# A two-layer streaming encoder step in float32: request packs of two pairs instead of one, and layer inputs that arrive already turned

## The reference

```python
for l in range(DEPTH):                         # 2 layers, for prompt and for requests
    P = rmsnorm(x, g_norm[l]) @ w_in[l]        # 1024 channels in
    o_a = sparse attention: an indexer keeps the top 256 (requests: 132) keys
    o_b = forgetting attention: logit[t,s] += F[t]-F[s], causal
    o_c = attention in a band of 8+1 chunks of 64, learned bias
    o_m = cross-attention into 256 memory tokens, kv = rmsnorm(mem, g_mem[l]) @ w_mem_kv[l]
    x = x + concat(o_a, o_b, o_c, o_m, each * silu(its gate)) @ w_out[l]
y = rmsnorm(x, g_final)                        # new keys and values are outputs too
```

## Time and profile before

| | us |
|---|---|
| median of 3 runs | 1713.91 |
| lowest, highest | 1713.59, 1715.81 |
| the profiled execution's own time | 1712.33 |
| its span, first to last instruction | 1710.5 |
| PE busy | 1692.7 |
| DVE busy | 1005.7 |
| ACT busy | 662.3 |
| POOL busy | 239.7 |

### The profile page before, as it was taken

How to read it: one execution, slowest core, us unless ns; L and a number is a source line. 1 busy time by engine, 2 the same in 40 slices (tenths; PEclk the granted TensorE clock), 3 DMA queues, 4 the chain that set the end, 5 groups by cost and what they waited for, 6 DMA issues and landing times.

```text
span 1710.5 us, 30251 instructions
## 1 busy us (share of the span) xinstructions
PE 1692.7 (99%) x10866; PEld 1103.7 (65%) x10866; DVE 1005.7 (59%) x2707; ACT 662.3 (39%) x1599; POOL 239.7 (14%) x452
## 2 busy tenths in 40 slices
PE   9999999999999999999999999999999999999998
PEld 4466677767778755555444677767777886555553
DVE  3645888778878333333235378887888772333321
ACT  4532334333343345454124323343333433445531
POOL 1233321100010010002012433220000001000000
PEclk9999999999999999999999999999999999999999
DMA  8344322223132322114421533231231324221130
GB/s 285 94 143 126 127 94 87 97 78 106 41 134 94 103 79 97 40 47 115 129 94 51 166 104 127 94 137 44 81 109 38 132 97 121 69 90 37 46 108 37
DMA packets 60340, 166.64 MB, mean 97 GB/s; under 512 B 11345, under 2 KB 29745, under 8 KB 57889
## 3 DMA queue, kind: packets, MB, share of 16 engines
q1 hardware_dynamic: 43584, 125.88, 23.0%
q0 software_dynamic: 16608, 38.83, 6.9%
HBM read 137.03 MB, written 30.73 MB: 98 GB/s over the span
## 4 chain that ended last, share of the span: by engine, by line
PE 80%; DVE 14%; DMA 2%; issue 2%; ACT 1%; DVEq 1%; ACTq 0%; SPq 0%
PE psX L876 54%; DVE lower L1268 9%; PE psT L816 7%; PE psX L1052 6%; PE psS L985 6%; DVE work L1490 2%; PE psS L904 2%; DMA wring<-in_w 2%; PE psS L816 1%; PE psX L816 1%; PE psX L1027 1%; DVE gate L1322 0%; PE psS L954 0%; PE psS L924 0%; DVE sc L1434 0%
## 5 line engine op out<-in xcount | busy, mean ns | idle before, releaser
L876 PE MATMUL psX<-wring,hT 128*128 128x512 f32 (+2 forms) x2016 | 834.3, 557 | 6.4 <-ACT kv L1146 3.0
L876 PEld LDWEIGHTS psX<-wring,hT 128*128 128x128 f32 x2016 | 363.9, 190 | 327.5 <-issue 318.6
L1268 DVE TENSOR_SCALAR_CACHE_REDUCE lower<-sc,thr 128x640 uint8<-128x640 f32 (+5 forms) x462 | 407.3, 934 | 17.5 <-issue 9.5
L876 PE MATMUL psX<-hT,wring 128*128 128x128 f32 x2880 | 334.6, 275 | 0.9 <-ACT gate L1166 0.4
L876 PEld LDWEIGHTS psX<-hT,wring 128*128 128x128 f32 x2880 | 327.7, 192 | 3.6 <-issue 3.0
L1208 ACT ACTIVATE work<-work,stat 128x256 f32<-128x256 f32 (+7 forms) x288 | 200.0, 694 | 295.9 <-DVEq L1493 293.3
L1217 ACT COPY work<-psT 128x512 f32<-128x512 f32 (+2 forms) x352 | 156.7, 488 | 321.0 <-PE psT L816 319.7
L816 PEld LDWEIGHTS psT<-con,work 128*128 128x128 f32 x1080 | 121.4, 141 | 73.2 <-issue 66.5
L816 PE MATMUL psT<-con,work 128*128 128x128 f32 x1080 | 158.2, 278 | 0.0
L1490 DVE CUSTOM_DVE_ANT_0 work<-psS,bias 128x640 f32<-128x640 f32 (+7 forms) x120 | 86.2, 718 | 41.9 <-issue 20.5
L1490 DVE CUSTOM_DVE_ANT_0 work<-psS,sc 128x384 f32<-128x384 f32 (+5 forms) x48 | 42.8, 891 | 72.1 <-PE psT L816 70.0
(11 more groups left out here) (203 smaller groups left out, 1537.9 us busy)
## 6 DMA issues: line engine op xcount, KB each, us to landing
wring<-in_w SPq DMA_DIRECT2D x17, 2048.0 KB, 9.4
cache<-in_kB SPq DMA_DIRECT2D x16, 512.0 KB, 7.0
cache<-in_vB SPq DMA_DIRECT2D x16, 512.0 KB, 4.1
cache<-in_kC SPq DMA_DIRECT2D x16, 512.0 KB, 6.8
cache<-in_vC SPq DMA_DIRECT2D x16, 512.0 KB, 4.7
scratch_oscr<-gate POOLq DMA_DIRECT2D x54, 128.0 KB, 2.0
hT<-scratch_oscr SPq DMA_DIRECT2D x18, 384.0 KB, 3.6
kv<-in_x SPq DMA_DIRECT2D x9, 512.0 KB, 5.7
```

The source lines that it names most:

```text
L876: mm = pe.matmul(out, lhs, rhs, start=(kt == 0), stop=(kt == KT - 1))
L1268: v.tensor_scalar(lower[:, at:at + STRIP_L[t]], sc[:, o], thr[:, n:n + 1], 0.0, ALU.is_lt, ALU.add, accum_out=below[:, n:n + 1])
```

## The change

Two things are changed.

First, a request pack now holds two pairs, requests four at a time: pair `j` goes to the first score buffer and pair `j+1` to the second, as even and odd heads do for the prompt. There are two request packs a branch instead of four; scores, values and `om` are written for both in one step, the queries of both pairs are prepared in one step on POOL, and the cache loads carry an index `i` for the pair. `sbias_` stays one buffer, so that between the two `L` of a B or A pack it is loaded anew.

Second, x of layer 0 and the memory tokens of both layers come a second time from the host, transposed (`xT`, `memT`), straight into `hT` and `memT`. There `norm` multiplies the turned tile by the gain per channel (DVE), and `turn` is one PE transpose of the reciprocal roots, spread over 128 columns, by which DVE multiplies the turned tile. The plain tiles are still loaded for the squares. The turned loads are `XT` steps of SP: x tiles 0, 1, 2, then 3 and 4, then 5 to 8, then the memory (6 in layer 0, one in layer 1). The two broadcast gain loads of 512 KB in layer 0, and one in layer 1, go.

```diff
+TURNED_IN = {"x0": range(0, 1), "x1": range(1, 2), "x2": range(2, 3), "x3": range(3, 5), "x5": range(5, 9), "m": range(9, 11)}
+def comes_turned(l, n):
+    return l == 0 or n > ST_
 def heads(pack):
-    return 1 if is_sample(pack) else pack[3]
+    return pack[3]
...
     emit("X", ("x", 0))
     emit("ident")
-    emit("gn")
+    emit("XT", "x0")
     emit("head")
     emit("X", ("x", 1))
+    emit("XT", "x1")
     emit("W", "A1")
+    emit("gm")
     emit("con")
     emit("X", ("x", 2))
+    emit("XT", "x2")
     emit("X", ("x", 3))
-    emit("gm")
+    emit("XT", "x3")
+    emit("XT", "x5")
     emit("W", "mm")
+    emit("XT", "m")
     emit("norm", 0)
...
                 queue += packs_of(c[0], t)
-                j = t
-                if c != "A2" and j < PAIRS:
-                    queue.append((c[0], f"s{j}", j, 1))
-        queue += [("A", f"s{j}", j, 1) for j in range(PAIRS)]
+                if c != "A2" and t in (1, 3):
+                    queue.append((c[0], f"s{t - 1}", t - 1, 2))
+        queue += [("A", f"s{j}", j, 2) for j in range(0, PAIRS, 2)]
...
-        gone = (l, ("turn", t)) if kind != "r" else (l + 1, ("turn" if l + 1 < DEPTH else "y", t))
+        gone = (l, ("norm", t)) if kind != "r" else (l + 1, ("turn" if l + 1 < DEPTH else "y", t))
...
         if l:
             put(at[(l, ("P", "A1", 0))], l, "gm")
+            put(at[(l, ("P", "A1", 0))], l, "XT", "m")
...
+                elif k == "XT":
...
+                        cols = slice(group[0] * P, (group[-1] + 1) * P)
+                        src = d["xT"].rearrange("p (k c) -> p k c", k=KT)
+                        sp.dma_start(hT[:, :, cols], src[:, :, cols]).then_inc(xT_loaded[s[1]].sem, 16)
...
+                    if comes_turned(l, n):
+                        turn(S.ap(s)[:, 0:P], rstd[:, 2, n:n + 1].to_broadcast([P, P])).then_inc(S.fill(s).sem, 1)
+                        continue
...
+                    if comes_turned(l, n):                       # DVE, norm
...
+                        dve.wait_ge(*xT_loaded[x].on(x))
+                        v.tensor_tensor(turned_tile(n), turned_tile(n), con[:, c0:c0 + KT].unsqueeze(2).to_broadcast([P, KT, P]),
+                                        ALU.mult)
+                        dve.wait_ge(*rooted.on(n))
+                        v.reciprocal(rstd[:, 2, n:n + 1], rstd[:, 1, n:n + 1]).then_inc(normed.sem, 1)
...
+                    if comes_turned(l, n):                       # DVE, turn
+                        roots = S.ap(s)[:, 0:P].unsqueeze(1).to_broadcast([P, KT, P])
+                        v.tensor_tensor(turned_tile(n), turned_tile(n), roots, ALU.mult).then_inc(S.empty(s).sem, 1)
...
+                elif k == "L" and is_sample(s[1]):               # POOL
...
+                    if br == "B":
+                        pool.wait_ge(*logits.on((p, i)))
...
+                        sample_bias(*sbias_loads[j + 1])
+                        if i == 0:
+                            close_samples("B", j + 1)
+                    elif br in "CA" and j + 1 < PAIRS:
+                        pool.wait_ge(*logits.on((p, i)))
+                        if br == "C":
+                            close_samples("C", j + 1)
+                        else:
+                            sample_bias("A", j + 1)
```

More of the change, by code:

```diff
@@ L172, in advance @@
             emit("S", pack)
-            if is_sample(pack) and pack[2] + 1 < PAIRS:
-                j = pack[2] + 1
-                emit("Q", (pack[0], f"s{j}", j, 1))
+            if is_sample(pack) and pack[2] + 2 < PAIRS:
+                j = pack[2] + 2
+                emit("Q", (pack[0], f"s{j}", j, 2))
         if prev:
@@ L205, in settle @@
             emit("V", pipe[1])
-        if old and is_sample(old) and old[2] == PAIRS - 1:
+        if old and is_sample(old) and old[2] + old[3] == PAIRS:
             emit("R", old[0])
@@ L411, in cache_uses @@
         elif s[0] in ("S", "V") and is_sample(s[1]):
-            out += [(l, (s, "k" if s[0] == "S" else "v", r)) for r in parts(s[1][0])]
+            out += [(l, (s, "k" if s[0] == "S" else "v", (i, r))) for i in range(s[1][3]) for r in parts(s[1][0])]
     return out
@@ L609, in encoder @@
         half_loaded = Signal(sem("half_of_b1_loaded"), [(l, "B1") for l in range(DEPTH)], lambda e: 16)
-        h_act = Signal(sem("hT_by_act"), events(["turn"], lambda s: s[1]))
+        h_act = Signal(sem("hT_by_act"), [(l, s[1]) for l, s in steps("turn") if not comes_turned(l, s[1])])
         h_dve = Signal(sem("hT_by_dve"), events(["turn"], lambda s: s[1]))
@@ L694, in merged, with turned_tile @@
             return gate[:, t, first * P:(first + n) * P].rearrange("p (g c) -> p g c", g=n)
+        def turned_tile(n, first=0):
+            if n > ST_:
+                return memT[:, first:, (n - 9) * P:(n - 8) * P]
+            return hT[:, first:, n * P:(n + 1) * P]
         def tile_of(l, n):
@@ L820, in scores_free @@
                 old = S.prior(use)
-                if old and old[1][0] == "turn":
+                if old and old[1][0] == "turn" and not comes_turned(old[0], old[1][1]):
                     pe.wait_ge(*h_act.on(old[1][1], old[0]))
@@ L1096, in _ @@
                                          scale=1.0 / D, bias=con[:, C_EPS:C_EPS + 1]).then_inc(rooted.sem, 1)
-                elif k == "turn":
+                elif k == "turn" and not comes_turned(l, s[1]):
                     n = s[1]
@@ L1100, in _ @@
                     src = S.ap(s)[:, 0:4 * P].rearrange("p (b c) -> p b c", b=4)
[L1101 to L1105 removed]
+                    nc.scalar.copy(hT[:, 0:4, n * P:(n + 1) * P], src)
                     act.drain().then_inc(h_act.sem, 1)
@@ L1708, in _ @@
                     p = s[1]
-                    br, _, j, _ = p
+                    br, _, j, n = p
                     if j == 0:
@@ L1718, in _ @@
                         pool.wait_ge(*S.fill(("is", PAIRS - 1)).on(("is", PAIRS - 1)))
-                    for hp in range(2):
-                        last = own_halves(queries(br), j, hp, slice(0, H), j % 2)
+                    for i in range(j, j + n):
+                        for hp in range(2):
+                            last = own_halves(queries(br), i, hp, slice(0, H), i % 2)
                     last.then_inc(qs_ready.sem, 1)
@@ L1832, in lay_out @@
     con, tmask = constants()
+    by_channel = lambda rows: a(rows.T.reshape(KT, P, -1).transpose(1, 0, 2).reshape(P, -1))
+    con[:, C_GT:C_GT + 3 * KT] = by_channel(np.stack([g_norm[0], g_mem[0], g_mem[1]]).astype(np.float32)
+                                            ).reshape(P, KT, 3).transpose(0, 2, 1).reshape(P, -1)
+    x = a(np.concatenate([x_prompt.reshape(SEQ, D), x_sample.reshape(P, D)]))
+    mem = a(mem_prompt.reshape(MEM, D))
     return {
-        "x": a(np.concatenate([x_prompt.reshape(SEQ, D), x_sample.reshape(P, D)])),
-        "mem": a(mem_prompt.reshape(MEM, D)),
+        "x": x, "xT": by_channel(x), "mem": mem, "memT": by_channel(mem),
         "w": a(w.reshape(-1, KT * 512)),
-        "gain": a(np.concatenate([np.stack([g_norm, g_mem], 1).reshape(2 * DEPTH, D), g_final[None]])),
+        "gain": a(np.concatenate([g_norm[1:], g_final[None]])),
         "bf": a(b_f),
```

210 lines of the change are left out of this document (107 added, 103 removed).

## The result

The changed kernel takes 1727.24 us (median of 4 runs, 1726.48 to 1727.65), the kernel before beside it 1713.75. The ratio is 1.0077, with a 95% interval of [1.0065, 1.0089]: slower by 13.5 us, outside the range of 1703.5 to 1720. The profiled execution took 1726.48 us with a span of 1724.7, 14.2 us more than before.

The account below looks back on a forecast made before the run. PE, busy 99% of the span, was taken to bound the kernel. Terms 0.0 + 1.5 - 1.7 - 2.0 + 0.5 = -1.7 us on the profiled 1712.33 gave 1710.6, or 1712.2 as a median; range 1703.5 to 1720.

Parts of the forecast that it names:

- Turns that shrink: PE, 11 turns in layer 0 and 2 in layer 1 become single transposes, saving 0.75 us each, 9.8 us in all.
- DVE's longer passes: DVE, turned input: some 0.6 us more a tile, hidden behind PE's unit; costed at 0, at worst 0.1 for three tiles.
- The wait for A1's weights: Start of layer 0: the rest lands at 15.6, PE's wait grows to some 2.5 us, eating the first three turns' gain.
- Tile 4: Layer 0, TR of A1 2: x tile 4 lands at 39.3 behind added loads, a new PE wait of 5.5 us.
- The clock behind it: PE after the tile 4 wait: may run at 1.2 GHz, costing 1.5 us, bounds 0 and 3.1.
- tile 4 comes in time: Rival, layer 0: loads land out of queue order or faster, the wait and clock term go, 1705.2 us; chance 0.16.
- Layer 1: Start of layer 1: two turns go for -1.5 us, the gain load's wait gives 0.2, sum -1.7 us.
- Request packs: Packs of two pairs: 16 merges save PE's step changes, 2.0 us; the bias reload costs 0.5.
- the bias reload: Between the two `L` of a B pack: DVE waits 2.3 to 4.4 us, costing +0.5 us, bounds 0 and 13; A 0.
- DVE sets the pace in B: Rival, B: the bias reload stops DVE and PE waits for nearly all, 1724 us, or half, 1718; chance 0.13.
- Small pieces cost far more: Rival, turned loads: small pieces at 200 GB/s, tile 4 lands at 44.4, 1717.3 us or above; chance 0.09.
- Merging worth more: Rival, request packs: six waits for ACT go and DVE does less, another -5 us, 1707 us; chance 0.12.

Follow-up runs that it names:

- input-only kernel: Kernel before with the turned input alone, request packs of one pair as before: 1716.00 us, ratio 1.0013.
- 1: Kernel before with request packs of two pairs alone, input loaded and turned as before: 1727.47 us, ratio 1.0085.
- 8: Packs of two pairs alone, with one bias shared by a pack's two pairs in A only, still reloaded in B: 1719.64 us, ratio 1.0035.
- number 4: Packs of two pairs alone, with the second pair in B and A using the first's bias, no reload between: 1712.28 us, ratio 0.9991.
- experiment 3: Turned input alone, with turned tiles 5 to 8 loaded behind tile 4, mm's weights and turned memory behind tile 5: 1710.21 us, ratio 0.9980.

## Why the prediction was wrong, step by step

**Turns that shrink: right; DVE's longer passes: not free.** In the input-only kernel PE's lag behind the kernel before falls by the 0.75 us forecast with each turn: at the last four matmuls of A1 units 5 to 7 it is 5.35, 4.59 and 3.88 us. But DVE's passes (1.22 us), which I cost at 0 (at worst 0.3 us), are not hidden for the last tile of x and the two of memory: PE waits 0.35, 0.72 and 0.45 us for them, 1.5 us in all. The forecast counted the 1.5 us that PE has left of the unit, and not what comes behind: index scores that need the score buffer which the pass reads.

**The wait for A1's weights: right in kind, too small.** I had the rest landing at 15.6; PE could start on it at 17.10, and the first part already was waited for (2.45 us at 11.00). Between 10 and 25 us the queue moved 335 to 383 GB/s, 360 on average, while I had taken 404 for all but the small pieces (307 and 375). The rate was not nearly constant in the kernel before either: 329, 416, 343 and 407 GB/s in the four windows from 5 to 25 us. And I priced the clock only behind tile 4: here, with two waits of 2.5 us, the twelve matmuls took 8.57 us instead of 5.09. In the changed kernel the wait for tile 4 takes most of this lateness up.

By the rule of the Trainium skill that I had set aside (DMA: Bandwidth & Descriptors, "Where 436 GB/s comes from": some 358 GB/s for traffic from HBM) those 360 come out right; in the same trace it is exceeded from 25 us on, with 408 to 413, and the kernel before moved 416 from 10 to 15 us.

**Tile 4: right in place.** Forecast to land at 39.3, it came at 41.7; the TR forecast at 43.0 ran at 45.50. The wait was 3.34 us and not 5.5, since PE itself came late. **The clock behind it: right in size.** 1.17 + 0.47 = 1.6 us were lost (2.87 for 1.70 us, 1.39 for 0.92, the latter pairs from the kernel with the loads moved), forecast 1.5. That was the middle of two bounds, 0 and 3.1, so the closeness is luck. The Trainium skill's rule (TensorE: Matmul & The Clock Gate, "HAM oscillation — how this bites in real kernels") would have had the whole 3.1. That PE starts slow behind a wait for a load is borne out at the start and behind tile 4; the price was 3.5 us for the two waits at the start together and 1.6 behind tile 4.

Together the first phase of layer 0 was to cost 0.0 + 1.5 us and cost 5.9: the TR came 2.5 us later than forecast, and DVE's passes took another 1.5. The rival "tile 4 comes in time" was wrong for the change as made. With the loads moved its wait and clock term do go: 5.8 us for the input alone, 5.3 for the whole change, where the rival had 7.0.

**Layer 1: right.** -1.7 forecast; in the input-only kernel the lag falls from 3.65 us at 871 to 1.64 at 912, -2.0: two turns for 1.5 and a wait of 0.93 us for 1.41. (At 975 it is 2.9 again, as PE waits 1.80 us for weights instead of 0.55.)

**Request packs: the step that failed.** The forecast's own sign of it is there: new waits of PE between 170 and 260 us, at 183.37 (1.36 us) and 195.63 (1.83). I had -2.0 for the merges and +0.5 for the bias reload, in sum -1.5; alone the packs cost 13.9. Two sentences of the forecast were wrong. "in A DVE has nothing else to do and PE's next need comes about 7 us later": DVE has the residual adds of the output units to do, they stand behind the waiting logits step in its order, and PE's accumulators wait for them. That is worth 8.3 us where I wrote 0. The profiled executions of 1 and 8 show where: 6.2 us more of waiting for these adds, and 4.4 us more for the twenty matmuls behind them, at a clock that had fallen (together more than the 8.3, as the profiled execution of 1 was 3.3 us above its median and that of 8 only 1.7). "PE needs those 3 us or more later, and the next iteration has no pack, so that DVE catches up": in B PE needed the score buffer at once. That is worth 6.9 us where I took 0.5 out of bounds of 0 to 13; with B's reload alone in the way, PE waits 5.1 us for these buffers, and the matmuls and turns behind the wait at 190.78 are 1.5 us slower than in layer 1. The rival "DVE sets the pace in B" had this mechanism, and its middle price, +6, is close to the 6.9. Its condition was that DVE's wait exceeds what PE has queued, about 3 us: a DVE wait of 2.19 us was already enough, as PE stood for 1.83 us of it. I gave it 0.13. What I weighed was DVE's own idle time; I did not ask for each instruction behind the wait which buffer it frees. And the gain of merging, 2.0, was 1.3 net (number 4) and nothing in C and M; the second pair needs a second score buffer at the same moment, for which PE waits 5.6 us in number 4.

**Small pieces cost far more** had tile 4 landing at 44.4; it came at 41.7, half way from the forecast to there. **Merging worth more** fell, although the six waits for ACT did go (3.0 to 0.7 us): others took their place.

## What to carry to other kernels

A step that is packed with its neighbour must find the buffers of both at hand: where one small operand is loaded between the two halves, the second half is late by a whole load, and what matters is what stands behind it on its engine and which accumulators and score buffers that frees. Loads that only a later phase needs go behind the first tile that the present one will miss, even if the queue seems to have room; experiment 3 moved three lines for 5.8 us. Check for each new wait of PE its clock price too, the short ones at the start included.

## What the runs showed of the hardware

PE's clock can fall behind waits as short as 2.5 us: in the changed kernel it is at 0.50 from 13 to 22 us, and six matmuls took 4.93 us instead of 2.53. It need not: in the input-only kernel the six behind a wait of 2.69 us ran at full clock (2.56 us), and it fell only in the next wait, of 3.56. In the middle of the program waits of PE for DVE did the same: ten matmuls took 5.94 to 7.40 us behind waits of 2.6 to 3.2 us instead of 4.46, so such a wait costs up to twice its length. Zeros in the waits kept the clock at 1.00, and still the median did not move (0.9979 against 0.9980), so a price seen in one profiled execution need not be one in the time. The load queue, with pieces of 512 B to 1 KB in it, moved 335 to 383 GB/s between 10 and 25 us, and 408 to 413 with those of 2 KB and the weights. The kernel before, without the small pieces, moved 416 and 407 in two of these three windows (in the third, 343, its engines were busy for 0.85 of the time), so the start of the program as such doesn't hold the queue back; that the small pieces do is likely and was not isolated.
